# Who adds the last squares of a norm: TensorE's ones matmuls against GpSimd's additions

## The reference

```python
def rms_norm(x, g):
    xf = x.astype(jnp.float32)
    y = xf * lax.rsqrt(jnp.mean(xf * xf, axis=-1, keepdims=True) + RMS_EPS)
    return (y * g.astype(jnp.float32)).astype(x.dtype)

x = x + g1 * rms_norm(y, post_mix_g)              # first block, after the mixer
h = rms_norm(x, pre_ffn_g) * (1.0 + sc2) + sh2    # input of its feed-forward network
x = x + g2 * rms_norm(y, post_ffn_g)              # first block's end
h = rmsnorm(x, norm1_g)                           # second block's input
h = rmsnorm(x, norm2_g)                           # input of the second feed-forward network
```

## Time and profile before

| | us |
|---|---|
| median of 3 runs | 2331.76 |
| lowest, highest | 2327.88, 2331.93 |
| the profiled execution, whole time | 2333.59 |
| its span in the trace | 2331.4 |
| PE busy in the span | 2221.8 (95%) |
| DVE, ACT, POOL busy | 1624.7 (70%), 1089.7 (47%), 908.5 (39%) |

### The profile page before, as it was taken

How to read it: one execution, slowest core, us unless ns; L and a number is a source line. 1 busy time by engine, 2 the same in 40 slices (tenths; PEclk the granted TensorE clock), 3 DMA queues, 4 the chain that set the end, 5 groups by cost and what they waited for, 6 DMA issues and landing times. The chain is left out here.

```text
span 2331.4 us, 29057 instructions
## 1 busy us (share of the span) xinstructions
PE 2221.8 (95%) x10136; PEld 1788.0 (77%) x10136; DVE 1624.7 (70%) x2175; ACT 1089.7 (47%) x1897; POOL 908.5 (39%) x651
## 2 busy tenths in 40 slices
PE   6999998998699999999997999999999999999999
PEld 4778886776588787878885767777778888887887
DVE  6458447627899999985788369994575555556685
ACT  5232256736444444454545458883343333334533
POOL 1130034414656656553014516662264434434310
PEclk9999999999899999999999999999999999999999
DMA  9156522034032323279964140003323323238986
GB/s 346 55 172 225 186 91 63 19 127 131 32 104 95 109 86 118 68 248 383 349 215 136 46 117 28 18 9 109 124 68 107 118 86 118 98 119 303 365 273 227
DMA packets 282565, 331.82 MB, mean 142 GB/s; under 512 B 18281, under 2 KB 180409, under 8 KB 282049
## 3 DMA queue, kind: packets, MB, share of 16 engines
q1 hardware_dynamic: 279760, 322.57, 40.9%
q0 software_dynamic: 2208, 7.37, 0.9%
q10 hardware_dynamic: 465, 0.17, 0.0%
HBM read 251.11 MB, written 78.94 MB: 142 GB/s over the span
## 5 line engine op out<-in xcount | busy, mean ns | idle before, releaser
L2629 PE MATMUL ps<-sum_hi,whi 128*128 128x512 f32 x640 | 250.1, 391 | 6.2 <-DVE cbuf L3348 6.2
L2630 PE MATMUL ps<-sum_lo,whi 128*128 128x512 f32 x640 | 249.5, 390 | 0.0
L2631 PE MATMUL ps<-sum_hi,wlo 128*128 128x512 f32 x640 | 249.4, 390 | 0.0
L2656 PE MATMUL ps<-sum_lo,whi 128*128 128x512 f32 x616 | 242.5, 394 | 5.3 <-DVE sum_lo L2839 3.0
L2658 PE MATMUL ps<-sum_lo,wlo 128*128 128x512 f32 x616 | 241.0, 391 | 0.0
L2657 PE MATMUL ps<-sum_lo,whi 128*128 128x512 f32 x616 | 240.9, 391 | 0.0
L2629 PE MATMUL ps<-hhi,whi 128*128 128x512 f32 x480 | 189.0, 394 | 20.1 <-DVE wlo L2796 16.0
L764 POOL TENSOR_TENSOR cbuf<-cbuf 128x512 f32<-128x512 f32 (+1 forms) x50 | 76.6, 1533 | 299.8 <-ACT cbuf L751 297.1
L226 DVE TENSOR_TENSOR wlo<-raw,whi 128x1024 fp32r<-128x1024 f32 x56 | 78.4, 1405 | 159.1 <-ACT whi L221 159.0
L2630 PE MATMUL ps<-hlo,whi 128*128 128x512 f32 x480 | 188.5, 393 | 0.0
L2631 PE MATMUL ps<-hhi,wlo 128*128 128x512 f32 x480 | 188.5, 393 | 0.0
(11 more groups left out here) (445 smaller groups left out, 5689.8 us busy)
## 6 DMA issues: line engine op xcount, KB each, us to landing
shared<-ffn_blocks SPq DMA_DIRECT2D x154, 256.0 KB, 5.2
lead_work<-in_w_down SPq DMA_DIRECT2D x105, 256.0 KB, 4.4
arena<-in_w_down SPq DMA_DIRECT2D x100, 256.0 KB, 4.0
raw<-in_w_up SPq DMA_DIRECT2D x36, 512.0 KB, 4.8
ffn_blocks<-chunk_work SPq DMA_DIRECT2D x66, 256.0 KB, 2.3
ffn_blocks<-lead_work SPq DMA_DIRECT2D x66, 256.0 KB, 2.3
raw<-in_w_in SPq DMA_DIRECT2D x32, 512.0 KB, 4.7
arena<-in_w_ada SPq DMA_DIRECT2D x32, 512.0 KB, 5.7
```

The costliest lines, as they stand in the source:

```text
L2629: nc.tensor.matmul(o, hi[:, ws], mhi, start=fresh and k == 0, stop=False, skip_group_check=True)
L2630: nc.tensor.matmul(o, hi[:, ws], mlo, start=False, stop=False, skip_group_check=True)
L2631: mm = nc.tensor.matmul(o, lo[:, ws], mhi, start=False, stop=(k == 3), skip_group_check=True)
L2656: nc.tensor.matmul(o, hi[:, ws], mhi, start=fresh, stop=False, skip_group_check=True)
```

## The change

POOL adds all eight squares in every round and half, and PE's sum is one matmul of the total. `n_total` becomes eight, `pe_sums` loses its loop, and the ranges in the three `pool` methods end at tile 7. Nothing else is touched; the slots and the order of the other engines stay.

```diff
             def n_total(self, r):
 
-                return DK - 1 if r == 0 else DK - 2
+                return DK
...
             def pe_sums(self, pe, r, h):
 
-                first = self.n_total(r)
-                pe.wait_ge(self.added[r], self.n_added(r, first - 1, h))
-                nc.tensor.matmul(self.sums(r, h), onesF[:, :], cbuf[:, self.slot(r, 0), half(h)], start=True, stop=False)
-                for k in range(first, DK):
-                    pe.wait_ge(self.squared[r], self.n_squared(r, k, h))
-                    mm = nc.tensor.matmul(self.sums(r, h), onesF[:, :], cbuf[:, self.slot(r, k), half(h)], start=False,
-                                          stop=(k == DK - 1))
-                mm.then_inc(self.summed[r], 1)
+                pe.wait_ge(self.added[r], self.n_added(r, DK - 1, h))
+                nc.tensor.matmul(self.sums(r, h), onesF[:, :], cbuf[:, self.slot(r, 0), half(h)], start=True, stop=True)\
+                  .then_inc(self.summed[r], 1)
...
                 self.lead.pool(pool)
-                norm.add_squares(pool, 0, 0, range(1, 7))
+                norm.add_squares(pool, 0, 0, range(1, 8))
                 norm.add_squares(pool, 1, 0, range(1, 4))
                 norm.add_squares(pool, 0, 1, range(4, 5))
-                norm.add_squares(pool, 1, 0, range(4, 6))
-                norm.add_squares(pool, 0, 1, range(5, 7))
-                norm.add_squares(pool, 1, 1, range(1, 6))
+                norm.add_squares(pool, 1, 0, range(4, 8))
+                norm.add_squares(pool, 0, 1, range(5, 8))
+                norm.add_squares(pool, 1, 1, range(1, 8))
...
-                tail.add_squares(pool, 0, 0, range(1, 7))
-                tail.add_squares(pool, 1, 0, range(1, 6))
-                tail.add_squares(pool, 0, 1, range(1, 7))
-                tail.add_squares(pool, 1, 1, range(1, 6))
+                tail.add_squares(pool, 0, 0, range(1, 8))
+                tail.add_squares(pool, 1, 0, range(1, 8))
+                tail.add_squares(pool, 0, 1, range(1, 8))
+                tail.add_squares(pool, 1, 1, range(1, 8))
...
-                self.norm.add_squares(pool, 0, 0, range(1, 7))
-                self.norm.add_squares(pool, 0, 1, range(4, 7))
+                self.norm.add_squares(pool, 0, 0, range(1, 8))
+                self.norm.add_squares(pool, 0, 1, range(4, 8))
```

## The result

| | us | ratio to before, 95% interval |
|---|---|---|
| before, median of 19 runs | 2330.13 | |
| after, median of 19 runs | 2335.54 | 1.0021 [1.0013, 1.0029] |
| forecast | 2337.0 on a median of 2331.76 | 1.0023 |

The change costs 0.21% of 2330 us, 4.9 us, between 3.0 and 6.8 by the interval (the medians lie 5.4 us apart); the forecast was 5.25 us. The runs of one kernel lie some 10 us apart (after: 2329.41 to 2339.64), and the profiled execution of after took 2330.45 us, less than that of before, 2333.59. It had already won 5.3 us before the first norm began, where the two kernels are alike. So the two traces can't be compared by their spans. They are compared by stretch: the same instruction is looked up in both, and what counts is by how much its distance to an earlier common instruction has grown.

A forecast was written before the change was run, and what follows sets the result against it. The norms' chains, not PE's work, were taken to bound the kernel. First norm +1.85, tail +2.6 and last norm +0.8 gave 5.25 us, so 2337.0 on 2331.76; own range 2335 to 2340, full range 2331 to 2341.5.

The forecast's parts named there:

- Three chains: At the three norms, the chain from squares to operand sets the time, not PE's work; changes arrive whole, +5.25 us.
- Rival three (PE decides): Whole kernel: PE's work sets the time, so all fourteen matmuls count, 12.2 us saved, 2319.6 us; chance 0.06.
- The first sum: First norm, round 0, first half: one matmul less brings the log 0.87 us earlier.
- Second sum and the meeting behind it: First norm, round 1, first half: log 0.6 us earlier, but additions delay DVE's scalings 0.9; +0.3 us in all.
- Last sum and the weight sums: First norm, round 1, second half: later additions cost +1.14 us, POOL's weight sums beside DVE's scalings +0.4.
- Round 1, first half: Tail: ACT's square and log +0.15 us, an addition meeting DVE's split +0.55; 0.7 us in all.
- Round 0, second half: Tail: a fourth POOL addition puts one more of DVE's operand instructions behind POOL, +0.9 us.
- Round 1, second half: Tail: the log comes 4.07 us after what was POOL's last addition instead of 3.08, +1.0 us.
- The first log: Last norm, first half: the sum starts at 1655.7 and the log comes at 1656.75, 0.65 us earlier.
- The second log: Last norm, second half: sum and log come at 1683.5 instead of 1682.93, +0.6 us.
- No meetings: Rival: POOL's additions slip between DVE's instructions, leaving the plain trade of +2.3 us, 2334.1 us; chance 0.32.
- The clock: Rival: PE's clock falls after three new idle times, adding 4.1 us at sums and tail products, 2341.1 us; chance 0.15.

The follow-up runs named there:

- fill: The changed kernel, plus 12, 9 and 10 small constant matmuls on PE before its waits at three second-half sums; 1.0023 of before.
- round 0 alone: Against before, POOL adds all eight squares in round 0 only; round 1 still leaves two squares to PE; 1.0006 of before.
- before's second trace: The kernel before, unchanged, executed and profiled once more; 2327.78 us.
- second trace of after: The changed kernel, not altered further, executed and profiled once more; 2339.67 us.
- Two more: The kernel before, with two unread POOL additions on spare data behind those of the tail's round 0, second half; 2329.36 us.
- mixed split: Against before, squares split between POOL and PE sum by sum, three left to PE where POOL is late, with a slot for round 1's last square; 0.9997.
- round 1 alone: Against before, POOL adds all eight squares in round 1 only; round 0 still leaves one square to PE; 1.0014 of before.

## Why the prediction was right

**The frame held, the total with some luck.** Three chains set the time, and what the change did to them arrived: 2.41 + 3.15 + 1.11 = 6.7 us in the trace of after, 4.9 (3.0 to 6.8) in the runs, 5.25 forecast. Behind the last norm's end nothing is won or lost for 385 us: there each kernel's lead or lag against before stays the same within 0.04 us. In the products from 2108 us to the end, though, the two traces of after came out 2.7 and 1.5 us shorter than before, fill 2.9 and round 0 alone 2.6. These are the three kernels that change the last norm's second sum; before's second trace and the four other kernels lie between 1.3 shorter and 0.3 longer. So the rival named for the second trace of after, that the units give back 1.5 us or more, may be true in part: 6.7 less 1.5 to 2.9 is 3.8 to 5.2. It may also be drift, for in the units before the tail kernels differ by −2.0 to +0.9 us without regard to the change. No run shows a cause, and the forecast had put this at nothing, so part of its closeness to 4.9 is luck. Rival three (PE decides) fell at once: PE lost 11.9 us of work and waits longer.

**First norm, +1.85 forecast, +2.41 found.** The first sum: −0.87 forecast, −0.86 found. Second sum and the meeting behind it: −0.6 + 0.9 = +0.3 forecast; found −0.45 at the log (from −0.86 to −0.45 against the first log, +0.41) and +0.84 up to the next, by an addition at 534.1 to 535.4 beneath the first scaling. Last sum and the weight sums: 1.14 + 0.4 = 1.54 forecast, 2.02 found. The parts were shared out otherwise: the log came 2.33 us later, 0.96 of it by the clock, and 0.31 came back at the weight sums; in fill, without the clock, 1.42 and another 0.57. The step that was mis-sized is this pair: they are no two costs to be added up, since the weight sums begin when the additions end, whatever the log does. And two more additions took 3.08 us and not the 2.88 priced (from 555.22 to 565.35 in after, 7.05 us before), with an idle time of 0.44 in their midst (561.27).

**Tail, +2.6 forecast, +3.15 found.** Round 1, first half: 0.7 forecast, 0.71 found up to its log. That figure holds some spread (0.47 in the second trace of after, 1.03 in fill); from the first split's start to the log it is +0.63 to +0.65 in all four traces in which POOL adds all eight for this sum. The size was right, the path was not. The split that the new addition met took 0.63 us longer (0.55 had been taken), but DVE's scalings wait 0.91 us for ACT in both kernels and would have hidden that. It arrived through POOL: the addition behind the split took 2.25 us instead of 1.61 (at 1230.52), and ACT's square and log, for which the forecast had 0.15, waited for it. Of the three additions read as lying beside the splits, only two did; the third lay beside the scalings. Round 0, second half: 0.9 forecast, 0.91 found, 0.88 in round 0 alone, 0.0 where it was undone. Two more shows that meeting by itself, at 0.77 each. Here the Trainium skill's rule (SBUF — State Buffer, Who interferes with whom), that a VectorE instruction with two inputs in SBUF and a GpSimd instruction that reads SBUF hold each other up, agrees with the trace: 1.63 us for a scaling of 0.75. Round 1, second half: 1.0 forecast, 1.53 found, 0.99 in fill: the rest is the clock (1.90 in the second trace of after, where the sum took 2.07 us).

**Last norm, +0.8 forecast, +1.11 found.** The first log: −0.65 forecast, −0.50 found from the square at 1637.70. The second log: 0.6 forecast, 1.64 found, and 0.53 of it given back by the end, as at the first norm. In the second trace of after and in fill, where that sum ran at the full clock, the log is 0.86 us late, counted from that square, and another 0.24 comes behind it (0.2 forecast): the same 1.1.

**The rivals.** "No meetings" (0.32) is out: every meeting of the list was found. The clock (0.15) did happen, at all three places in the first trace of after and at two in the second, which the forecast had not taken for the likeliest. It was no alternative to the forecast but came on top of it. It was priced at 4.1 us in all; the logs lost 0.96, 0.56 and 0.80 us, of which POOL's weight sums took back the first and the last, so that 0.5 us (0.9 in the second trace) stayed, in the tail. The products behind the tail's norm, priced at 1.5 us, only used up PE's wait (1.55 us before, 0.50 after, at 1273.19). The whole times of after and fill can't tell so little. The argument "idle 1.55 and 0.59 us are short" was beside the point: the new idle times were 2.37 to 3.64 us, and in this range the sums ran slow in most executions and not in all. Apart from the split's path the forecast was right in its steps, and too low in each stretch by 0.3 to 0.6 us: by the clock in the tail, by the additions ahead of the log and POOL's sums behind it in the other two.

## What to carry to other kernels

To move work from the busiest engine to the idlest is a loss where the idle engine stands last in a chain that the busy one waits for: read at each place who waits for whom, and choose by place. An instruction on GpSimd holds VectorE up where both work from SBUF, though nothing waits for it (0.77 to 0.9 us for one of 1.3 here); put such work where VectorE works from PSUM or is idle. And where a sum stands in the midst of another engine's queue, its place must be moved with the work: the mixed split brought nothing until the sum came earlier.

## What the runs showed of the hardware

In after, idle times of 2.37, 2.60 and 3.64 us were followed by sums of two passes that took 1.69, 1.93 and 2.08 us, at a granted clock that fell to the lower level; after 1.86 us (at 531.81) the sum took 1.13 us. How long PE was idle does not settle it by itself: the second trace of after has 1.12 us after 2.60, round 1 alone 1.13 after 2.75 in the first norm and 2.07 after 2.37 in the tail. Small products of constants in the idle time, leaving 1.05, 0.41 and 0.38 us of it, kept two passes at 1.12 to 1.13 us and the granted clock at 1.00. The start of the last norm took 1.3 us more or less in executions of the same kernel (before, twice), which no change of these kernels explains, while stretches that start behind that step repeat within 0.01 us: a stretch must be seen in several executions before a microsecond of it is called an effect.
